# A two-layer hybrid decoder on one core: query projection with four head tiles on other weight slots, V turned later, boundary tasks reordered, mask and maximum fused

## The reference, cut to what matters

```python
h = h + rms_norm(mamba2_mixer(rms_norm(h, a_norm_pre), ...), a_norm_post)      # boundary 0 behind it
h = h + rms_norm(conv_ffn(rms_norm(h, f_norm_pre[0]), ...), f_norm_post[0])    # boundary 1 behind it
k, v = rms_norm(h, kv_norm) @ w_kv                                             # 4 tiles of 128 columns
q = rms_norm(h, b_norm_pre) @ w_q                                              # 8 tiles of 128 columns
s = where(mask, q . k, NEG_INF); p = softmax(concat(s, sink))                  # window 128 + 16 meta tokens
h = h + rms_norm((p . v) @ w_o, b_norm_post)                                   # boundary 2 behind it
h = h + rms_norm(conv_ffn(rms_norm(h, f_norm_pre[1]), ...), f_norm_post[1])    # boundary 3, the end
```

## Time and profile before

| | |
|---|---|
| median of 3 runs | 2553.01 us (2552.59 to 2553.37) |
| the profiled execution: its time | 2555.75 us |
| its span | 2554.1 us |
| mean granted clock of TensorE | 0.988 of full speed |
| PE busy | 2490.9 us (98%) |
| DVE busy | 1625.3 us (64%) |
| ACT busy | 1168.8 us (46%) |
| POOL busy | 592.9 us (23%) |
| chain that ended last | PE 81%, DVE 6%, ACT 4% |

### The profile page before, as it was taken

The page is one execution under the profiler, slowest core; times in us unless marked ns, Lnnn a source line. Parts: engine busy times, 40 slices in busy tenths (PEclk is TensorE's granted clock), DMA queues, the critical chain, the costliest instruction groups (busy, mean ns, idle before and its releaser), DMA issues.

```text
span 2554.1 us, 45758 instructions
## 1 busy us (share of the span) xinstructions
PE 2490.9 (98%) x18254; PEld 1738.5 (68%) x18254; DVE 1625.3 (64%) x2183; ACT 1168.8 (46%) x2174; POOL 592.9 (23%) x401
## 2 busy tenths in 40 slices
PE   8999999999999999999999999899999999999998
PEld 5676676667655677777766666676656777877665
DVE  6776868696867877777412385694379777773123
ACT  5455655655425544444211254595355444442121
POOL 1012112122151123222211111254411223221221
PEclk9999999999999999999999999998999999999999
DMA  3122223222132121211312012000121111213111
GB/s 119 62 92 79 83 84 98 77 87 87 49 111 100 50 63 36 66 49 49 136 46 72 13 40 61 34 2 9 42 108 50 58 50 49 66 56 124 46 56 66
DMA packets 67806, 167.68 MB, mean 66 GB/s; under 512 B 5680, under 2 KB 37840, under 8 KB 67408
## 3 DMA queue, kind: packets, MB, share of 16 engines
q1 hardware_dynamic: 67664, 165.70, 19.4%
HBM read 151.76 MB, written 12.86 MB: 64 GB/s over the span
## 4 chain that ended last, share of the span: by engine, by line
PE 81%; DVE 6%; ACT 4%; issue 4%; POOLq 2%; DVEq 1%; POOL 1%; ACTq 1%; DMA 0%
PE PS L2190 21%; PE PS L2191 20%; PE PS L2192 20%; PE PS L2579 4%; PE PS L2577 4%; PE PS L2578 4%; PE PS L2454 1%; PE PS L2461 1%; ACT BIG L1479 1%; DVE TT L1636 1%; PE PS L2443 1%; ACT BIG L1492 1%; DVE UB L1574 1%; POOLq L752 1%; PE PS L2284 1%
## 5 line engine op out<-in xcount | busy, mean ns | idle before, releaser
L2190 PE MATMUL PS<-R,whi 128*128 128x384 f16 (+2 forms) x2400 | 747.8, 312 | 2.6 <-DVE wlo L1539 1.6
L2191 PE MATMUL PS<-R,whi 128*128 128x384 f16 (+2 forms) x2400 | 747.4, 311 | 0.0
L2192 PE MATMUL PS<-R,wlo 128*128 128x384 f16 (+2 forms) x2400 | 747.2, 311 | 0.0
L2190 PE MATMUL PS<-BIG,whi 128*128 128x384 f16 (+2 forms) x1452 | 451.5, 311 | 6.6 <-issue 4.5
L2191 PE MATMUL PS<-BIG,whi 128*128 128x384 f16 (+2 forms) x1452 | 451.4, 311 | 0.0
L1539 DVE SCALAR_TENSOR_TENSOR wlo<-stage,whi 128x1024 f16<-128x1024 f32 (+1 forms) x150 | 206.0, 1375 | 385.6 <-ACT whi L854 384.8
L2192 PE MATMUL PS<-BIG,wlo 128*128 128x384 f16 (+2 forms) x1452 | 451.3, 311 | 0.0
L2190 PEld LDWEIGHTS PS<-R,whi 128*128 128x128 f16 x2400 | 236.0, 98 | 127.3 <-issue 13.4
L2191 PEld LDWEIGHTS PS<-R,whi 128*128 128x128 f16 x2400 | 236.0, 98 | 122.3 <-issue 11.0
L2192 PEld LDWEIGHTS PS<-R,wlo 128*128 128x128 f16 x2400 | 236.1, 98 | 118.5 <-issue 2.0
L854 ACT ACTIVATE whi<-stage 128x1024 f16<-128x1024 f32 (+1 forms) x150 | 164.4, 1110 | 148.4 <-PE PS L2192 129.2
(11 more groups left out here) (270 smaller groups left out, 4393.9 us busy)
## 6 DMA issues: line engine op xcount, KB each, us to landing
stage<-wa SPq DMA_DIRECT2D x164, 512.0 KB, 3.5
stage<-wd SPq DMA_DIRECT2D x32, 704.0 KB, 4.1
TT<-cs_rows SPq DMA_DIRECT2D x32, 512.0 KB, 3.7
h_keep<-hT SPq DMA_DIRECT2D x2, 4160.0 KB, 12.6
EC<-cs_rows SPq DMA_DIRECT2D x64, 128.0 KB, 3.7
hT<-h SPq DMA_DIRECT2D x4, 1536.0 KB, 10.4
hT<-h_keep SPq DMA_DIRECT2D x4, 1536.0 KB, 8.4
out<-hT SPq DMA_DIRECT2D x4, 768.0 KB, 3.5
```

The lines of the kernel that those rows point to most:

```text
L2190: eng.matmul(acc, WH[slot][:, ws], xh, start=first, stop=False)
L2191: eng.matmul(acc, WH[slot][:, ws], xl, start=False, stop=False)
L2192: return eng.matmul(acc, WL[slot][:, ws], xh, start=False, stop=last)
```

## The change

Four edits are made together, all of them in order and placement except the last one.

1. **Query projection.** The first four tiles are done block by block instead of the first two; tiles 0 and 1 take the weight slots 2 and 3 in AUX, tiles 2 and 3 the slots 0 and 1. The 18 V turns start behind pair 5 instead of pair 0, in another order of windows, two of them behind each of the pairs 12 to 16.
2. **Boundaries 0 and 2** (`TAIL[p] == 4`). On ACT the last square of a block (`square_last`) is taken out of `close` and put behind `keep_strips` and `pre` of the block before; the third and fourth weight split go between the squares of o1; the steps of o1 up to `split_x` stand ahead of the heads' evacuation, and `post` of o2 behind them. On DVE the third split's low part goes into the residual update of o1. On PE head 2 of o0 stands ahead of `mean_pre` of o1, and `mean_post` of o2 goes into head 0 of o1.
3. **Attention's start.** The first scores wait for all but the last two evacuations, and the waits for V move behind the first transposes.
4. **Attention's rounds.** The three DVE instructions of `masked` become four fused ones, one for each head, that write the negated masked scores and their minimum; ACT's exponential takes scale -1. The copy of the turned own keys moves from ACT to DVE (`own_copy`), that of the previous keys stays on ACT. Two semaphores take the place of one, and `max_ready` that of `scores_masked`.

```diff
-Q_SEQ = [(i, b) for b in ORD for i in range(2)] + [(i, b) for i in range(2, KD) for b in range(3)]
+Q_HEAD = {ORD[0]: (0, 1, 2, 3), ORD[1]: (0, 1, 2, 3), ORD[2]: (2, 3, 0, 1)}
+Q_SEQ = [(i, b) for b in ORD for i in Q_HEAD[b]] + [(i, b) for i in range(4, KD) for b in range(3)]
+V_AT = {c: (c - 5,) for c in range(5, 12)}
+V_AT.update({c: (2 * c - 17, 2 * c - 16) for c in range(12, 17)})
+V_AT[17] = (17,)
...
+                def square_last(b):
+
+                    s, n = span(b, LO_POST[p])
+                    eng.wait_ge(mix_sq_summed, 3 * p + ORD.index(b) + 1)
...
+                    eng.activation(T1[:, s:s + n], cut(mix(KD - 1, b), b, LO_POST[p]),
+                                   ACT.Square).then_inc(mix_sq_last, 1)
...
-                    close(o1, tiles[1:])
+                    close(o1, tiles[1:], False)
                     keep_strips(q_, o0)
                     pre(q_, o0)
+                    square_last(o1)
                     split_x(q, o0, range(4))
...
                     post(p, o1)
-                    squares(q_, o1)
-                    close(o2, tiles[2:])
+                    close(o2, tiles[2:3])
+                    turned(KD - 2, o2)
+                    hi(u_next + 2)
+                    squares(q_, o1, range(4))
+                    close(o2, tiles[3:], False)
+                    turned(KD - 1, o2)
+                    hi(u_next + 3)
+                    squares(q_, o1, range(4, KD))
+                    keep_strips(q_, o1)
+                    pre(q_, o1)
+                    split_x(q, o1, range(3))
+                    square_last(o2)
+                    split_x(q, o1, range(3, KD))
+                    post(p, o2)
...
-                    post(p, o1, mix)
+                    post(p, o1, mix, lambda: lo(u_next + 2), 2)
+                    lo(u_next + 3)
...
             boundary(1, 2, mix_r1, U_KV, k_low=k_low)
             k_low(ORD[1])
-            pre(3, ORD[0])
+            pre(3, ORD[0], lambda: lo(U_Q, aux=True))
             k_low(ORD[2])
-            lo(U_Q)
-            lo(U_Q + 1)
-            pre(3, ORD[1])
+            lo(U_Q + 1, aux=True)
+            pre(3, ORD[1], lambda: lo(U_Q + 2))
+            lo(U_Q + 3)
             pre(3, ORD[2])
...
-                eng.tensor_tensor(z[:, :, 1:1 + w], score_acc(n, 0, w), mask[0:T, :].unsqueeze(1).broadcast_to([T, QPK, w]),
-                                  ALU.add).then_inc(scores_masked, 1)
-                eng.drain()
-                eng.tensor_reduce(soft(n, 0), z, AX.X, ALU.max)
-                eng.drain()
-                eng.tensor_scalar(soft(n, 1), soft(n, 0), -1.0, None, ALU.mult).then_inc(max_ready, 1)
+                z, a = logits(n), score_acc(n, 0, w)
+                for r in range(QPK):
+                    o = eng.tensor_tensor_reduce(out=z[:, r, 1:1 + w], in0=a[:, r, :], in1=mask[0:T, 0:w], scale=-1.0,
+                                                 scalar=pr[0:T, C_SINK + QPK * g + r:C_SINK + QPK * g + r + 1],
+                                                 op0=ALU.add, op1=ALU.min, accum_out=soft(n, 1)[:, r:r + 1])
+                o.then_inc(max_ready, 1)
...
+            def own_copy(n):
...
+                eng.wait_ge(probs_turned, n + 1)
+                if n > 1:
+                    eng.wait_ge(values_ready, n - 1)
+                pt = PTS[n % 2].rearrange("p (a m) -> p a m", a=2)
+                eng.tensor_copy(pt[0:own, 1, 0:QPK * T], PS[0:own, 5, 0:QPK * T]).then_inc(own_copied, 1)
...
                 if n > 1:
                     out_lo(n - 2)
+                own_copy(n)
...
                 head(0, o0)
                 head(1, o0)
...
+                if g == 4:
+                    head(2, o0)
                     mean_pre(p + 1, o1)
...
+                    head(3, o0, 0, 2)
                     strips_sum(p + 1, o1)
...
+                    head(3, o0, 2)
+                    head(0, o1, 0, 5)
+                    mean_post(p, o2)
+                    head(0, o1, 5)
+                    head(1, o1)
+                    head(2, o1)
+                    mean_pre(p + 1, o2)
+                    head(3, o1, 0, 2)
+                    strips_sum(p + 1, o2)
+                    head(3, o1, 2)
...
-            eng.wait_ge(evac, 6 + 3 * (J_Q + KD))
+            eng.wait_ge(evac, 6 + 3 * (J_Q + KD) - 2)
```

More of the change, by code:

```diff
@@ L481, in program, with q_next @@
         V_WIN = [(QB * b, own_keys(b)) for b in range(NQB)] + [(QB * c - META, P) for c in range(1, NQB - 1)]
+        V_ORDER = list(range(3, NQB)) + [0, 1, 2] + list(range(NQB, len(V_WIN)))
+        def q_next(i, b):
+            return i >= 4 and b == 2 or i in (2, 3) and b == ORD[2]
         def v_rows(c):
@@ L1050, in turned, with close @@
                     eng.wait_ge(acc_ready, 3 * j0 + tail_pos(p, m, b) + 1)
-                def close(b, ms):
+                def square_last(b):
+                    s, n = span(b, LO_POST[p])
+                    eng.wait_ge(mix_sq_summed, 3 * p + ORD.index(b) + 1)
+                    if p == 0:
+                        eng.wait_ge(out_b, tail_pos(p, KD - 1, b) + 1)
+                    else:
+                        eng.drain()
+                    eng.activation(T1[:, s:s + n], cut(mix(KD - 1, b), b, LO_POST[p]),
+                                   ACT.Square).then_inc(mix_sq_last, 1)
+                def close(b, ms, last=True):
                     s, n = span(b, LO_POST[p])
                     for m in ms:
-                        if p == 0 and m < KD - 1:
+                        if p == 0 and (m < KD - 1 or not last):
                             continue
@@ L1062, in close @@
                         a = PS[:, tail_pos(p, m, b) % 6, 0:n]
-                        if m == KD - 1:
+                        if m == KD - 1 and last:
                             eng.wait_ge(mix_sq_summed, 3 * p + ORD.index(b) + 1)
@@ L1469, in _ @@
                 r.then_inc(kq_hi, 1)
-                if c < len(V_WIN):
-                    v_copy(c)
-                if b == (ORD[2] if i < 2 else 2):
+                for j in V_AT.get(c, ()):
+                    v_copy(j)
+                if q_next(i, b):
                     hi(U_Q + i + 2)
@@ L1551, in post @@
                 for k in range(KD + 1):
-                    if between is not None and k == 5:
+                    if between is not None and k == at:
                         between()
@@ L2717, in _ @@
                 scores(n)
+            eng.wait_ge(evac, 6 + 3 * (J_Q + KD))
             for n in range(NQD):
```

131 lines of the change are left out of this document (71 added, 60 removed).

## The result

The changed kernel takes 2527.98 us (median of four runs, 2525.64 to 2528.8), the kernel before 2553.19 on the same chip (2552.59 to 2553.9). The ratio is 0.99, 95% interval [0.9883, 0.9917]. The forecast was 2529, faster. The profiled execution of the changed kernel took 2525.64 us.

A forecast was written before the change was run, and what follows sets the result against it. PE was 98% busy, so only its gaps and lowered clock could be won. Boundary 0 -5.5, boundary 2 -4.5, query projection -7 and attention -7 give -24, from 2553.0 to 2529 us; range 2519 to 2545.

The forecast's parts named there:

- Boundary 0, -5.5 taken: Boundary 0: reordering removes two PE stalls at the strips' copy; 5.5 us faster, bounds -9 to 0.
- The hand sum: Boundary 0: head 0 of o2 ends near 821.7 instead of 828.2, a gain of 6.5 us at full clock.
- The 1 us taken off for the clock: Boundary 0: 1 us deducted because PE waits ahead of `mean_pre` of o1 and then runs in short pieces.
- The rival in which half clock eats the boundaries' gain: Boundaries: PE gets half clock in heads 0 of o1 and o2, so they give nothing; 2539 us, chance 0.15.
- Boundary 2, -4.5 predicted: Boundary 2: strips' sum 5 us earlier, head 0 of o2 gains 4.6 by boundary 0's chain; bounds -7 to 0.
- Query projection, -7 predicted: Query projection: 12.3 us of old waits and low clock go, 4.3 of new waits and 1 for clock come.
- 5.9 us of which half, 2.9, are lost: Query projection: after the 3.53 us V wait PE runs at half clock for 5.9 us, losing 2.9.
- Attention's rounds, 5.9 predicted: Rounds 4 to 35: 3.244 us falls to 3.05, where PE's work and the copy loop meet; 5.9 us gained.
- the lower bound of 0.43: Attention's mask: a fused instruction with its accumulator's write takes 0.43 us if instructions overlap, 0.59 end to end.
- the break-even of 2.1: Attention's rounds: a masked block of 2.1 us, 0.53 a pair, makes DVE's round equal 3.05 us.
- the second rival: Attention's mask: the fused instruction runs at half rate, block 3.4 us, round 4.4; 2571 us, chance 0.07.
- 1.5 us were predicted up to round 4: Attention's start: shorter 128-key blocks and no `exps` wait for turned keys in rounds 2 and 3 gain 1.5 us.

The follow-up runs named there:

- x_bound_old: The changed kernel with boundaries 0 and 2 in their old order of work; 2537.25 us.
- after: The profiled execution of the changed kernel itself, with no further edit; 2525.64 us.
- after_again: The changed kernel with no edit, run and profiled again beside the kernel with both later edits; 2529.71 us.
- x_better: The changed kernel with the edits of x_query_lows and x_att_start together; 2525.63 us.
- both_old: The changed kernel with both boundaries and the query projection in their old form, the attention's edits kept; 2543.9 us.
- x_query_lows: The changed kernel with low parts of query tiles 1 and 2 ahead of DVE's input task of o1, tile 3's inside it; 2527.17 us.
- x_query_old: The changed kernel with the query projection and V's turns in their old order and weight slots; 2536.73 us.
- x_scores_half: The changed kernel with scores from the high part of K alone, 8 matmuls a round instead of 16; one profiled execution, 2521.96 us.
- x_mask_old: The changed kernel with the mask in three unfused DVE instructions again, the own-key copy still on DVE; 2547.22 us.
- x_att_start: The changed kernel with DVE's last low part behind the second mask and the sinks' negation in the query projection; 2529.13 us.

## Why the prediction was right

**Boundary 0, -5.5 taken, 6.6 measured** (6.7 in x_bound_old). The hand sum gave 6.5. Its terms as written end at 821.1 and not at 821.7, which would be 7.1; head 0 of o2 was through 74.4 us behind `mean_post`, and these two are 74.1 and 74.7, so the sum held within 0.3 us either way. The first place came 2.6 us earlier (15.27 behind `mean_post` against 17.92), as said. The second sum of strips came 43.66 us behind `mean_post` (788.53 - 744.87) against 49.71 (796.72 - 747.01), 6.05 us earlier where 5.2 were worked out; head 0 of o1 ran in waiting pieces as said. The 1 us taken off for the clock is the part to look at. In "after" the clock was 1.00 throughout; in after_again the same wait of 0.75 us in head 0 of o2 was followed by a fall, and the stage lasts 688.55. These windows are the same stretch of the two (2.66 us apart):

```profile
816.00:820.00 4.00, 2.90 (x22) 1.86 (x23) 3.77 (x11) 2.81 (x6) 0.78 (x1) 1.00 0.34 137
```

```profile
819.00:823.00 4.00, 3.25 (x16) 2.05 (x17) 3.77 (x10) 2.81 (x6) 0.78 (x1) 0.66 0.02 4
```

Of ten profiles with the new boundary four lost 1.4 to 1.6 us so (688.5 to 688.7 in the table), three at this place and x_better at head 0 of o1. The rival in which half clock eats the boundaries' gain exists, at some 1.5 us instead of the 10 that it was given. By the pair that is compared the stage gains from 3.4 us (both_old to x_better) to 6.7.

**Boundary 2, -4.5 predicted, 3.7 measured.** The strips' sum came 42.89 behind `mean_post` (1843.42 - 1800.53) against 46.89, 4.0 us earlier, not 5, and again without a wait:

```profile
1843.42 0.81 PE L2347 MATMUL PS<-TT,stripsum 128*128 128x384 f32 x2
```

The term was over-sized by carrying boundary 0's chain over whole. The two differed in the kernel before: there the clock fell behind both waits of boundary 0 (1.65 us for each sum in the earlier trace rows) and only behind the second of boundary 2 (0.91 and 1.44 in the earlier trace rows).

**Query projection, -7 predicted, 5.3 to 8.5 measured.** The waits were 1.3 + 2.3 + 0.9 = 4.5 us where 0.6 + 2.6 + 1.1 = 4.3 had been worked out from DVE's queue (the first was twice its size, the others smaller), and x_query_lows shows that the first two, 3.6 us, are DVE's order; the third stayed with 1.0 us. No clock was lost behind them, so the 1 us added for it was not due. What the edit is worth depends on which execution it is measured against: 5.3 us by x_query_old, of which 4.50 + 2.39 + 0.4 - 4.5 = 2.8 are waits and the rest, 2.5, the low clock from 1522.6 to 1530 (0.50, then 0.71 to 0.73); some 3 us more, 10.7 - 2.2 = 8.5, against the profiled execution of before, whose clock stood at half behind the V wait. The step that was mis-sized is "5.9 us of which half, 2.9, are lost": it was true of that execution; in both_old and x_query_old the wait at the same place, 2.4 us there, passed without it. How many executions of the kernel before have it is open.

**Attention's rounds, 5.9 predicted, 6.7 measured, and both bounds as said.** A round was to be 3.05 us. It is 3.03, from PE's own work, and x_scores_half shows the loop over ACT's copy only 0.09 us behind it, so "both meet" held. The fused pair takes 0.40 us, below the lower bound of 0.43. The fused instruction itself takes 0.48, more than the 0.42 worked out; but the read of its accumulator, for which 0.09 were added, costs nothing, since it lies beside the next one. The rest of DVE's round was put at 0.93 and is 0.96 in x_mask_old. The old block of 2.67 lies past the break-even of 2.1, and with it the rounds are 3.55, from DVE; no run has a block near 2.1 itself.

The Trainium skill (VectorE: DVE Perf Modes, Two Vector instructions with no wait between them) counts such an operation as two instructions of which the next starts early. The trace agrees: the read of the accumulator takes 0.08 us and starts with the next fused instruction, both 0.40 us behind the last.

The half rate of the second rival did not come. A fused instruction on 128 elements takes 0.35 us and one on 256 takes 0.48, so 128 elements more cost 0.13 us, 1.0 ns each, as for the plain form:

```profile
1614.28 0.35 DVE L2185 CUSTOM_DVE_ANT_0 BIG<-PS,BIG,pr 112x128 f32<-112x128 f32 x1
```

The Trainium skill (Vector Engine (DVE) Microarchitecture Reference, Points that are easy to get wrong) halves the rate of the scalar-tensor-tensor form for two non-bf16 sources in SBUF. Here one source is in PSUM, so this run neither bears it out nor refutes it for the fused instruction.

**Attention's start.** 1.5 us were predicted up to round 4, and 1.1 were won: from the end of the projection's last product to round 4 it is 2.23 + 17.79 = 20.0 us before and 18.9 after. Edit 3 had no part in the first half of it. PE starts its first scores 2.2 us earlier and then waits 4.4 us for the first masks, where it waited 2.23 + 1.15 + 0.59 = 4.0 in three places; the first transposes come 8.55 us behind the projection before and 8.51 after. The prediction said so ("DVE is busy until then anyway"), though the first mask comes 0.5 us later than before (4.2 us behind the projection against 3.7), and two blocks of 128 keys are 0.5 us shorter (1.09 against 1.63) where 0.2 for each were predicted. The 1.1 us lie between the first transposes and round 4; no run separates the moved waits for V from edit 4 there. It is DVE that stands in the way of the first mask:

```profile
1612.41 1.23 DVE L1575 SCALAR_TENSOR_TENSOR wlo<-stage,whi 128x1024 f16<-128x1024 f32 x1
1613.55 0.37 DVE L2171 TENSOR_SCALAR pr<-pr 128x16 f32<-128x16 f32 x1
1614.06 0.20 DVE L2182 COPY BIG<-pr 128x4 f32<-128x4 f32 x1
```

A low part, the negation of the sinks and a copy stand ahead of the first mask, and PE waits 4.41 us for it, from 1611.10 to 1615.51. The rest of that time is DVE too: two evacuations, 1.1 us together, from 1611.26 on, and 1.1 of the fused instructions. x_att_start moves the low part and the negation. The wait falls to 2.73 + 0.59 us, but the next one, for POOL's division at the first transposes, grows from 0.73 to 1.64, and 0.7 us are won at round 4.

Behind round 35 the changed kernel is 1.3 us faster (0.6 in executions with the longer end): four more rounds lie there, for which the prediction had no term.

**The total.** 25.2 us between the medians against 24 predicted. The sum of the stages without "to b0" is 28.0 with "after" and 26.6 with after_again, of which 3 are the half clock behind the V wait in the profiled execution of before, the one that took 2555.75 us against the median of 2553. The waits went, and the new ones came, where the prediction put them, so the mechanism was right in its main terms. That the total came within 1.2 us is partly luck: boundary 2 was 0.8 too high, boundary 0 (1.1) and the attention (2.1 with its end) too low, the query projection depends by 3 us on the execution, and executions of one kernel scatter by as much.

## What to carry to other kernels

Two edits to one loop can be worthless or harmful apart and pay together: work out each engine's round with both, and look for where the bounds meet, since beyond that point nothing more is to be had. When a wait is taken away, go through the queue of the engine that fed it and price the next item that is late; here that gave 4.3 us of 4.5 and showed where the next 4 us were. Compare kernels by stages between fixed rows, not by spans, when unchanged code moves by more than the effect.

## What the hardware showed that was not expected

Unchanged code up to boundary 0 took 744.6 to 749.8 us in 13 profiles. The clock is at least part of the reason. Windows of the changed kernel in its two profiles, first "after", then after_again, around the same unchanged place:

```profile
109.00:113.00 4.00, 4.00 (x19) 1.90 (x17) 1.55 (x4) 0.67 (x2) 0.00 (x0) 0.60 0.62 222
...
538.00:542.00 4.00, 4.00 (x29) 2.79 (x28) 3.69 (x7) 3.93 (x12) 0.00 (x0) 1.00 0.62 189
```

```profile
109.00:113.00 4.00, 4.00 (x15) 1.99 (x14) 1.28 (x2) 0.31 (x1) 0.00 (x0) 0.50 0.60 236
...
538.00:542.00 4.00, 4.00 (x21) 2.33 (x20) 3.21 (x5) 3.83 (x11) 0.00 (x0) 0.70 0.41 138
```

Near 534 us PE waits 0.62 us in the one and 0.60 in the other; the first keeps 2.4 GHz, the second has a mean of 0.87 in 534 to 538 and 0.70 in the window shown, so it ran at 1.2 GHz for part of them. By these means it loses 0.5 + 1.2 = 1.7 us (an estimate). The two waits end 0.96 us apart (533.58 and 534.54) and boundary 0 begins 2.66 apart, so this one fall is the difference between the two places. Waits of 2.3 and 2.4 us kept the full clock (the query projection of "after", x_query_old, both_old), waits of 3.53 and 4.5 us were followed by the half one, and so were those of 2.54 and 2.31 us in the earlier trace rows and that of 0.75 in after_again. The first wait of the earlier trace rows, 1.96 us, kept it, and those of 4.4 us at the attention's start did not (0.50 behind it in "after"). The length of a wait alone therefore doesn't tell whether the clock falls; what else decides it stays open. For a forecast, the clock behind a short wait is a chance of one to three us, not a price.
